# A decoder trunk on one core: order of the pieces inside and between mLSTM heads

## The reference

```
q = block_diag(xc, w_q); k = block_diag(xc, w_k) * HD ** -0.5; v = block_diag(xm, w_v)
S = (q k^T) * exp(D - m_t)                      # causal, D from the gates
num = inter * (q C) + S v;   den = inter * (q . n) + sum(S)
h = num / max(|den|, exp(-m_t))                 # then RMS norm over the head
C_new = scale * C + (k * w_s)^T v;   n_new = scale * n + sum(k * w_s)
```

## Time and profile before

| | |
|---|---|
| runs | 1950.24, 1951.23, 1963.34 us; median 1951.23 |
| profiled execution | 1950.55 us, span 1948.8 us, mean granted TensorE clock 0.987 |
| busy: TensorE | 1892.1 us (97% of the span) |
| busy: VectorE, ACT, POOL | 738.7 (38%), 723.8 (37%), 778.2 (40%) |
| chain that ended last | TensorE 86%, VectorE 5% |
| HBM | 167.57 MB read, 40.64 MB written |

### The profile page before, as it was taken

How to read it: one execution, slowest core, us unless ns; L and a number is a source line. 1 busy time by engine, 2 the same in 40 slices (tenths; PEclk the granted TensorE clock), 3 DMA queues, 4 the chain that set the end, 5 groups by cost and what they waited for, 6 DMA issues and landing times.

```text
span 1948.8 us, 35952 instructions
## 1 busy us (share of the span) xinstructions
PE 1892.1 (97%) x13703; PEld 1752.8 (90%) x13703; DVE 738.7 (38%) x868; ACT 723.8 (37%) x1062; POOL 778.2 (40%) x663
## 2 busy tenths in 40 slices
PE   7999999999999999999999999999999999999997
PEld 7999999999999999997554554999999999999997
DVE  6677632111110132697656667222221111101214
ACT  4576733322222235434242242423433322212342
POOL 3233554543554544473110100554545545544441
PEclk9999999999999999999899999999999999999998
DMA  4222232222222223222668578222323222222222
GB/s 126 81 83 82 87 95 77 78 89 82 81 85 83 81 80 78 84 83 80 208 226 306 199 241 289 88 87 65 96 80 84 83 82 81 83 85 76 86 78 69
DMA packets 187147, 209.70 MB, mean 108 GB/s; under 512 B 24475, under 2 KB 150051, under 8 KB 186991
## 3 DMA queue, kind: packets, MB, share of 16 engines
q1 hardware_dynamic: 186818, 208.19, 34.7%
q10 hardware_dynamic: 224, 0.07, 0.0%
HBM read 167.57 MB, written 40.64 MB: 107 GB/s over the span
## 4 chain that ended last, share of the span: by engine, by line
PE 86%; DVE 5%; issue 4%; ACT 2%; POOL 2%; DMA 1%; SPq 0%; DVEq 0%; POOLq 0%; ACTq 0%
PE ps L2196 72%; PE ps L2444 2%; PE ps L2505 2%; PE ps L2542 2%; POOL W_LO L660 1%; PE ps L2483 1%; PE ps L2560 1%; PE ps L2378 1%; PE ps L2493 1%; DVE H_PAD L1680 1%; DVE C_HALVES L2004 1%; DVE K_T L1875 1%; PE ps L2516 0%; DMA X_ROWS<-in_x_prompt_dram 0%; PE ps L2367 0%
## 5 line engine op out<-in xcount | busy, mean ns | idle before, releaser
L660 POOL TENSOR_TENSOR W_LO<-W_RAW,W_HI 128x512 fp32r<-128x512 f32 x464 | 625.9, 1358 | 737.4 <-ACT W_HI L960 737.0
L960 ACT ACTIVATE W_HI<-W_RAW 128x512 fp32r<-128x512 f32 x484 | 298.9, 629 | 707.3 <-PE ps L2196 707.0
L2196 PE MATMUL ps<-A_HI,W_HI 128*128 128x288 f32 x2304 | 496.4, 297 | 13.8 <-POOL W_LO L660 5.3
L2196 PE MATMUL ps<-A_HI,W_LO 128*128 128x288 f32 x2304 | 495.2, 297 | 0.0
L2196 PE MATMUL ps<-A_LO,W_HI 128*128 128x288 f32 x2304 | 494.8, 296 | 0.0
L2196 PEld LDWEIGHTS ps<-A_HI,W_HI 128*128 128x128 f32 x2304 | 372.7, 189 | 16.1 <-issue 13.8
L2196 PEld LDWEIGHTS ps<-A_HI,W_LO 128*128 128x128 f32 x2304 | 372.9, 190 | 0.0
L2196 PEld LDWEIGHTS ps<-A_LO,W_HI 128*128 128x128 f32 x2304 | 372.6, 189 | 0.0
L1762 DVE TENSOR_TENSOR X<-X,ps 128x1152 f32 (+1 forms) x36 | 48.8, 1354 | 312.2 <-PE ps L2196 312.2
L2196 PE MATMUL ps<-G_HI,W_HI 128*128 128x288 f32 x768 | 164.5, 296 | 0.5 <-DVEq L1788 0.5
L2196 PE MATMUL ps<-G_LO,W_HI 128*128 128x288 f32 x768 | 164.5, 296 | 0.0
(11 more groups left out here) (383 smaller groups left out, 2297.1 us busy)
## 6 DMA issues: line engine op xcount, KB each, us to landing
W_RAW<-in_ffn_w_up_dram SPq DMA_DIRECT2D x176, 256.0 KB, 2.8
C_HALVES<-in_state_mlstm_C_dram SPq DMA_DIRECT2D x64, 512.0 KB, 5.0
out_ml_C_s_dram<-C_HALVES SPq DMA_DIRECT2D x64, 512.0 KB, 5.4
W_RAW<-in_ffn_w_down_dram SPq DMA_DIRECT2D x88, 256.0 KB, 2.6
W_RAW<-in_ml_w_in_dram SPq DMA_DIRECT2D x64, 256.0 KB, 2.8
W_RAW<-in_rg_w_in_dram SPq DMA_DIRECT2D x48, 256.0 KB, 2.8
W_RAW<-in_ple_w_gate_dram SPq DMA_DIRECT2D x32, 256.0 KB, 2.7
W_RAW<-in_ml_w_out_dram SPq DMA_DIRECT2D x32, 256.0 KB, 2.8
```

Source lines behind the costliest of these rows:

```text
L660: pool.tensor_tensor(W_LO[:, s], W_RAW[:, s], W_HI[:, s].bitcast(F32), ALU.subtract).then_inc(lo_ready, 1)
L960: act.activation(W_HI[:, s], W_RAW[:, s], ACT.Copy).then_inc(hi_ready, 1)
L2196: ins = pe.matmul(ps[:, 4 * s + 2 * m + h, 0:HALF_T], a[:, w, k, wc], x[:, h * HALF_T:h * HALF_T + HALF_T], start=i == 0 and k == 0 and q ...
```

## The change

It reorders pieces and renames banks; no matmul, copy or DMA is added or taken out.

1. Unit 3 stands ahead of `pv3` (the fourth weighted values).
2. VectorE's `denominators` is split: `sample_denominators` (the four instructions on `ds`) and `prompt_denominators` (two on `den`), both between `update(h, 3)` and `update(h, 4)`.
3. `qs` and `ks` of head h + 1 are made in head h, behind unit 6, and copied by ACT there. `cn` (with its copy, now `prompt_normaliser`) stands ahead of them; before it followed unit 7.
4. In heads 1 to 3 the value stack `vs` goes ahead of the key projection `kt`. VectorE adds squares of `hn` ahead of the key copies.
5. ACT runs the next head's exponentials ahead of the `cp3` copy. POOL's `key_tokens` waits in addition for `nt` of the head before.

```diff
-    tail = [("u2", UNIT_BANKS), ("ds", (1,)), ("pv2", (2,)), ("pv3", (3,)), ("n0", (0,)), ("u3", UNIT_BANKS), ("den", (2,)),
-            ("u4", UNIT_BANKS), ("cp0", (3,)), ("u5", UNIT_BANKS), ("cp1", (1,)), ("hp", (2,)), ("u6", UNIT_BANKS), ("cp2", (2,)),
-            ("n1", (0,)), ("u7", UNIT_BANKS), ("cn", (3,)), ("cp3", (1,)), ("nt", (3,))]
+    tail = [("u2", UNIT_BANKS), ("ds", (1,)), ("pv2", (2,)), ("n0", (0,)), ("u3", UNIT_BANKS), ("pv3", (3,)), ("den", (2,)),
+            ("u4", UNIT_BANKS), ("cp0", (3,)), ("u5", UNIT_BANKS), ("cp1", (1,)), ("hp", (2,)), ("u6", UNIT_BANKS), ("cn", (3,))] \
+        + [("next qs", (1,)), ("next ks", (2,))] * (h + 1 < HEADS) \
+        + [("cp2", (3,)), ("n1", (0,)), ("u7", UNIT_BANKS), ("cp3", (1,)), ("nt", (2,))]
...
-    return [("qt", UNIT_BANKS), ("qs", (0,)), ("ks", (1,)), ("v0", (2,)), ("v1", (3,)), ("kt", UNIT_BANKS), ("vs", (0, 1)), ("v2", (2,)),
+    return [("qt", UNIT_BANKS), ("v0", (3,)), ("v1", (2,)), ("vs", (0, 1)), ("kt", UNIT_BANKS), ("v2", (2,)),
             ("hn", (3,)), ("st", (4, 5)), ("v3", (2,)), ("v4", (3,)), ("sc0", (1,)), ("u0", UNIT_BANKS), ("sc13", (2,)), ("sc2s", (3,)),
...
                 pool.wait_ge(bank_freed[bank], FREED[h, "ks", bank])
+                pool.wait_ge(piece_done, DONE[h - 1, "nt"])
...
-                prompt_state(h, 3)
+
+            def sample_end(h):
+
                 if h + 1 < HEADS:
                     exps_(h + 1)
+                prompt_state(h, 3)
...
-                    query(h, 0)
-                    query(h, 1)
-                    sample_columns(h, "ks", K_T)
-                    sample_columns(h, "qs", Q_T)
-                    query(h, 2)
-                    query(h, 3)
+                    for c in range(4):
+                        query(h, c)
...
                 root_mean(h, "hp", 0, SEQ)
+                prompt_normaliser(h)
+                if h + 1 < HEADS:
+                    sample_columns(h + 1, "qs", Q_T)
+                    sample_columns(h + 1, "ks", K_T)
                 prompt_state(h, 2)
...
+                    add_squares(h - 1, N_Q[:, :, :], squares_s, sums_s)
                     for c in range(4):
                         key(h, c)
-                    add_squares(h - 1, N_Q[:, :, :], squares_s, sums_s)
                     old_queries(h)
                     v_stack_lo(h)
                     square_mean(h - 1, "hn", 0, SEQ, N_STOK)
...
                 update(h, 3)
+                sample_denominators(h)
+                prompt_denominators(h)
                 update(h, 4)
                 add_squares(h, Q_T[:, :, 0:SEQ], squares_p, sums_p)
-                denominators(h)
                 update(h, 5)
...
+                unit(h, 3)
                 weighted(h, 3)
-                unit(h, 3)
                 denominators(h)
...
                 unit(h, 6)
+                prompt_sums(h)
+                if h + 1 < HEADS:
+                    sample_projection(h + 1, "q")
+                    sample_projection(h + 1, "k")
                 prompt_state(h, 2)
                 unit(h, 7)
-                prompt_sums(h)
                 state_and_numerators(h)
```

More of the change, by code:

```diff
@@ L83, in head_order @@
                 ("r0", (2,)), ("r1", (3,)), ("r2", (1,)), ("r3", (2,)), ("pv0", (3,)), ("u1", UNIT_BANKS), ("pv1", (1,))] \
-            + [(name, {"ds": (2,), "pv2": (3,), "pv3": (1,), "den": (3,), "cp0": (1,), "hp": (3,), "cp1": (2,), "cp2": (3,), "cn": (1,),
-                       "cp3": (2,), "nt": (1,)}.get(name, banks)) for name, banks in tail]
-    return [("qt", UNIT_BANKS), ("qs", (0,)), ("ks", (1,)), ("v0", (2,)), ("v1", (3,)), ("kt", UNIT_BANKS), ("vs", (0, 1)), ("v2", (2,)),
+            + [(name, {"ds": (2,), "pv2": (3,), "pv3": (1,), "den": (3,), "cp0": (1,), "hp": (3,), "cp1": (2,), "cp2": (1,), "cn": (1,),
+                       "next qs": (2,), "next ks": (3,), "cp3": (3,), "nt": (2,)}.get(name, banks)) for name, banks in tail]
+    return [("qt", UNIT_BANKS), ("v0", (3,)), ("v1", (2,)), ("vs", (0, 1)), ("kt", UNIT_BANKS), ("v2", (2,)),
             ("hn", (3,)), ("st", (4, 5)), ("v3", (2,)), ("v4", (3,)), ("sc0", (1,)), ("u0", UNIT_BANKS), ("sc13", (2,)), ("sc2s", (3,)),
             ("u1", UNIT_BANKS), ("r0", (1,)), ("r1", (2,)), ("r2", (3,)), ("r3", (1,)), ("pv0", (2,)), ("pv1", (3,))] + tail
-PIECES = [(h - 1 if name == "hn" else h, name, banks) for h in range(HEADS) for name, banks in head_order(h)] + [(HEADS - 1, "hn", (4,))]
+PIECES = [(h + {"hn": -1, "next qs": 1, "next ks": 1}.get(name, 0), name.split()[-1], banks)
+          for h in range(HEADS) for name, banks in head_order(h)] + [(HEADS - 1, "hn", (4,))]
 BANKS = {(h, name): banks for h, name, banks in PIECES}
@@ L1353, in square_denominators, with prompt_normaliser @@
                 act.activation(SCALE_F, DEN, ACT.Square, scale=EPS ** 0.5).then_inc(den_squared, 1)
-            def sample_end(h):
+            def prompt_normaliser(h):
                 bank = at(h, "cn")
@@ L2021, in add_squares, with sample_denominators @@
                 dve.tensor_tensor(sq[:, 0], sq[:, 0], sq[:, 3], ALU.add).then_inc(out, 1)
[L2023 to L2031, removed]
+            def sample_denominators(h):
+                bank = at(h, "ds")
                 dve.wait_ge(piece_done, DONE[h, "ds"])
@@ L2038, in denominators, with prompt_denominators @@
                 dve.wait_ge(bank_freed[bank], FREED[h, "ds", bank])
-                dve.wait_ge(bank_freed[dbank], FREED[h, "den", dbank])
+            def prompt_denominators(h):
+                bank = at(h, "den")
+                if h == 0:
+                    dve.wait_ge(rows_spread, 16)
+                dve.wait_ge(piece_done, DONE[h, "den"])
+                link(dve.scalar_tensor_tensor(DEN[:, 0:SEQ], ps[:, bank, :], -1.0, EXP_NEG_M[:, 0:SEQ], ALU.mult, ALU.max))
+                dve.tensor_tensor(DEN[:, 0:SEQ], ps[:, bank, :], DEN[:, 0:SEQ], ALU.max).then_inc(bank_freed[bank], 1)
+                dve.wait_ge(bank_freed[bank], FREED[h, "den", bank])
             bank = at(0, "cols")
@@ L2626, in _ @@
                     projection(h, "q")
-                    sample_projection(h, "q")
-                    sample_projection(h, "k")
                     value(h, 0)
                     value(h, 1)
+                    value_stack(h)
                     projection(h, "k")
-                    value_stack(h)
                     value(h, 2)
```

## The result

| | before | after |
|---|---|---|
| median of 12 runs each | 1951.02 us (1947.56 to 1966.05) | 1939.8 us (1929.93 to 1945.52) |
| profiled execution | 1950.55 us, span 1948.8, clock 0.987 | 1940.70 us, span 1939.0, clock 0.988 |

A forecast was written before the change was run, and what follows sets the result against it. TensorE, busy for 97% of the span, was taken as the bound. Denominators 12.6 us + boundaries 0.3 - a late load 0.2 = 12.7 us off the profiled 1950.55 gives 1937.9, stated as 1938; 8-in-10 range 1933 to 1946.

The forecast's parts named there:

- Denominators early: Sample denominators ahead of update 4: four waits before `cp1` go, 7.6 us, plus slow stretches behind three, 5.0: 12.6 us.
- Rival F: Half clock at `cp1` doesn't hang on the gap: slow `cp1`s stay, 5.0 us not won, 1943 us; chance 0.04.
- alone the shorter head would have run into it: Unit 7's last load in head 2, landing near 1130.2, would come late unless moved pieces delay unit 7 to 1131.3.
- rival B: State loads become the bound: units 6 and 7 wait, taking back most of the gain, about 1946 us; chance 0.10.
- Unit 3: Ahead of `pv3`, state stores and loads start about 2 us earlier; head 0's unit 6 load still 0.2 us late.
- Moved pieces: Sample projections (1.84 us) and `cn` between units 6 and 7: nothing won by themselves, but they cover unit 7's load.
- The boundary: `qt` to first scores, 13.60 to 11.65 us, 1.84 of it merely moved: 0.1 us saved at each of three boundaries.
- Rival A: New boundary stalls, 0.3 + 1.1 us, drop the clock, up to 1.7 us each: 1943 us; chance 0.19.
- Rival C: Boundary comes out clean, value and key copies earlier than worked out: 3 x 1.4 us more, 1934 us; chance 0.11.
- POOL: Earlier masks and key tokens slow VectorE's normalisation and square additions: 0 to 2.1 us over three boundaries, taken as 0.
- rival D: Late next-head rows stop ACT's queue ahead of `cp3` and `nt` copies, delaying queries and keys: about 1956 us; chance 0.03.
- The end: Behind head 3, TensorE's 3.20 us wait for the first weight split: 0 to 0.9 us effect, taken as 0.

The follow-up runs named there:

- den_late: Changed kernel with both denominator parts put back behind update 4 and the additions of squares: 1954.39 us, ratio 1.0018 to the kernel before.
- den_early_alone: Kernel before with only VectorE's denominators split and moved between updates 3 and 4: 1957.19 us, ratio 1.0040 to the kernel before.
- no_cover_u7: Changed kernel with `cn` back behind unit 7 and the sample projections back behind `qt`: 1953.88 us, ratio 0.9994 to the kernel before.
- den_early_again: Kernel before with only the denominators split and moved early, run once more for a second trace: 1964.67 us, one execution.
- pv3_first: Changed kernel with unit 3 put back behind `pv3`: 1940.68 us, ratio 0.9944 to the kernel before.
- best1: Changed kernel with the value stack back behind the key projection and `v4` in bank 6: 1936.00 us, ratio 0.9930 to the kernel before.
- best2: best1 with ACT's first four weight splits ahead of its `cp3` copy and `cn` behind unit 7, both in head 3: 1933.73 us, ratio 0.9907.
- v4_bank6: Changed kernel with value rows `v4` of heads 1 to 3 in bank 6 instead of bank 3: 1936.86 us, ratio 0.9927 to the kernel before.
- after_again: Changed kernel, unaltered, once more on another chip for a second trace: 1938.65 us, ratio 0.9934 to the kernel before.

## Why the prediction came out right

**Denominators early: right, on a condition it had named too weakly.** All four gaps and all slow `cp1`s went, 12.6 us as summed; den_late brings both back. Rival F is refuted: `cp1` is at full clock four times without its gap, and with it takes 5.40 us again in two heads of den_late. The Trainium skill ("TensorE: Matmul & The Clock Gate", HAM oscillation) has only longer gaps as harmful and would have left the 5.0 us; the runs here disagree, 3.70 against 5.40 us. The condition was in one sentence, "alone the shorter head would have run into it". The prediction priced a lost cover at the wait, rival B at 8 us in all; den_early_alone and no_cover_u7 show 6.9 and 3.6 us of waits and then a stretch of 20.5 and 23.9 us at half clock, den_early_again two of 23.9. Without that cover the change would have come out level with the kernel before (no_cover_u7), a case that had no chance of its own in the forecast.

**Unit 3: right.** No load wait in heads 1 to 3. Head 0's unit 6 is 0.2 us late, the value taken (its load was issued at 967.02 and took 5.6 us, the unit starts at 972.74); on another chip units 5 and 6 lost 0.9 together. For unit 7 of head 2 the last load to land ahead of it was issued at 1117.16 and took 5.3 us: 1122.5, 2.4 us ahead of the unit (1124.89), where 1.1 had been worked out. Counted from the start of `cp1` without its gap, SyncE issued it 1.4 us earlier than before (4.5 against 5.9 us behind it). The sum had left that out of its line; pv3_first, 6.4 us, shows that it is the effect of unit 3's place.

**Moved pieces: right as cover, with two costs missed.** `cn` and `cp2` now share bank 3, in head 3 with nothing between them: `cp2` waits 0.26 us for ACT's copy of `cn`. And the clock fell once behind them (`cp2` 5.35 us in head 1), 1.7 us, without a gap. That is more than a chance of this execution: of the eight traces that have `cn` and the sample pieces ahead of `cp2`, four show a slow `cp2` in one head (after, best1, best2, pv3_first).

**The boundary: right almost to the tenth.** 11.57 us against 11.65; `v4` waits 1.06 against 1.1; key rows 0.32 against 0.3; query copies end 3.40 us behind `qt` against 3.5; key copies start at 6.17 against 6.28. Saved, 13.60 - 11.57 - 1.84 = 0.19 us each, 0.6 in all against 0.3. Rival A, that this wait costs clock, did not happen: TensorE's granted clock from 1133 to 1145 us was 1.00, and `sc0` takes 3.70. Rival C, the boundary without the new wait, is what v4_bank6's trace measures: 1.1 us each less, about 3 in all.

**POOL: the slowdown came, and its price was the 0 taken.** Normalisation lost 1.88 us beside POOL's 1.94 us of copies; the reciprocal kept its 3.34 us beside POOL's masks. The Trainium skill ("SBUF — State Buffer", Who interferes with whom) has a VectorE instruction with two SBUF inputs contend with a GpSimd instruction that reads SBUF, and one with a single SBUF input not; the rows agree with both. The 0.74 us that VectorE still waits for the keys is what is left of the cover, and part of that is luck: the masks start 1.6 us ahead of `qt` where before they came 2.6 behind it, 4.2 us earlier and not 2.6, and so only the copies fell on instructions that they slow.

**ACT (rival D): the exponentials ended at 987.79, 1.7 us ahead of `qt`,** where "about at its start" was forecast. Of the difference 1.2 us are the table load, which ran before e_ready had come; most of the rest is e_ready itself, 3.1 us ahead of `qt` and not 2.5.

**The end and the sum.** The wait there grew by 0.1 us, inside the bound. The heads gave 12.6 + 0.6 - 0.2 - 0.3 - 1.7 = 11.0 us by these terms, 11.5 by the starts; 0.5 is unexplained. Behind them 2.0 us are lost, 0.8 at the first weight jobs and 1.2 near 1318 us, where the change touches nothing; 0.35 us had been gained ahead of unit 2 of head 0. "No half-clock stretch" up to the weight jobs was wrong by the one in head 1. Near 1318 after_again shows no such stretch, so the 1.2 us differ between two executions of one kernel. At the first weight jobs all fourteen traces, before included, have the clock at half behind the wait; from the first job to `hn` of head 3 it takes 14.2 to 15.6 us (before 14.4, after 15.1, after_again 14.9, den_late 14.2), and whether the change lengthens it or chance does is not shown. The changed kernel's own runs differ by 15.6 us at mean clocks from 0.987 to 0.991, and the order of the times doesn't follow the clock, so part of that spread stays open too.

## What to carry to other kernels

When a wait of TensorE goes, look for the transfers that had been landing inside it, and move some TensorE work in front of them in the same edit; the half that removes the wait alone can be a loss. Price a missed cover by what the clock does behind the wait, not by the wait: here 1.9 and 2.1 us of waiting in the middle of the heads cost 11 and 10 us more. And at a hand-over between stages, a bank given to a new piece is a wait for the whole queue of the engine that frees it, so try another bank first.

## What the runs showed of the hardware

- **A wait followed by pieces of few columns.** Behind a unit 7 that had waited 1.37, 1.94, 2.06 or 2.21 us and was followed by `cn` (one column) and the tail of `cp3` and `nt` (32 to 512 columns), the granted clock was 0.50 for 20.5, 23.9, 23.9 and 23.9 us. The same kernels also showed waits of 1.80 and 1.77 us in that place without it, and 0.76 or less there never did it. Before a long run of 512 columns (`cp1`), a gap of 1.9 or 2.0 us cost 1.7 us at most. Whether it takes the wait, the small pieces or both is not shown, as no run changed one of them alone. In head 3 (1.37 and 2.21) the wait for the first weights lies inside the stretch, and it cost 6 and 8 us instead of 10 and 11.
- **Clock behind small pieces.** `cp2` took 5.35 us behind 2.8 us of pieces with 1 and 64 columns in head 1 of after, with no gap, and 3.65 or 3.70 in the other three heads. Head 1 of best2 shows the same; best1 (head 0) and pv3_first (head 2) show 5.35 and 5.52 us where unit 6 had waited 0.89 and 0.68 us ahead of these pieces.
- **ACT loads its table ahead of a wait.** In after the load starts at 982.23, while the exponentials it serves begin at 986.38; before, the load of head 2 to 3 started at 1140.26, right behind a copy. These are the exponentials before, right behind the load, and ACT's rows of after:

```profile
1141.55 1.27 ACT L1307 ACTIVATE PROBS<-PROBS 128x1280 f32<-128x1280 f32 x1
```

```profile
982.23 1.28 ACT L1310 ACT_TABLE_LOAD   x1
986.38 1.27 ACT L1310 ACTIVATE PROBS<-PROBS 128x1280 f32<-128x1280 f32 x1 [2.87 <-DVE RG_STATE_IN L1961]
```
